# Mixing the values ahead of the gate step in every attention turn

## The chip, the cores and the metric

One core of one Trainium2 chip runs the whole kernel. The metric is the device time of one launch in microseconds, as the median of several runs. Times inside the kernel are read from one profiled execution.

## The reference

Two network blocks stand one behind the other, on 1024 positions of width 1024, in float32. The first block (a convolution mixer and a feed-forward part) and the pooling layer of the second block come before the part that matters here. That part is the attention layer of the second block: 16 query heads of 64 channels, 2 heads of keys and values, a window of 128 positions, a bias by distance and a sink for each head.

```python
q, z = jnp.split(h @ w_in, 2, axis=-1)
q = q * (HEAD_DIM ** -0.5)
...
s = jnp.einsum('bqhgd,bkhd->bhgqk', qn, kn).astype(jnp.float32) + pos_bias
s = jnp.where(mn[None, None, None], s, NEG_INF)
m = jnp.maximum(jnp.max(s, axis=-1, keepdims=True), sink)
p = jnp.exp(s - m)
p = p / (jnp.sum(p, axis=-1, keepdims=True) + jnp.exp(sink - m))
return jnp.einsum('bhgqk,bkhd->bqhgd', p.astype(vn.dtype), vn)
...
return (o * jax.nn.silu(z)) @ w_out
```

So three things come together: the scores and their softmax, the mixing of the values with the probabilities, and the gate z, which is a plain product of the normed stream h with weights.

## The kernel before

The kernel is written with explicit engine programs. Each of TensorE, VectorE, ScalarE, GpSimd and SyncE has its own list of instructions, and they meet only at semaphores (`wait_ge`, `then_inc`). An engine does its list strictly in the written order. A plain product is made of three matmuls for each 128 rows of the contraction (high part by high part, high by low, low by high), 512 columns each.

Attention is cut into 32 windows: for each of the two heads of keys and values, 16 query windows of 64 positions. A loop `for u in range(32 + 4)` on each engine is a pipeline over them. In turn u TensorE does, in this order:

- `scores(u)` (line 1469): 8 matmul instructions, into banks 4 to 7.
- In turns 0 to 2 a tile of queries, `query_pair`.
- `gate_step(n)` for n = u (lines 1453 to 1455): one eighth of a gate tile, three matmuls into bank 3. In turns 4 to 7 there are two such steps, so that from turn 8 on the step number is the turn. A tile is full after eight steps, at the end of the gate steps of turns 7, 15, 23 and 31. The first step of a tile waits until ScalarE has read the tile before (`act_read`).
- `mix_values(u - 4)` (line 1497): four matmuls of 512 columns into bank 2 (two in windows whose first chunk of keys is hidden: windows 0, 1, 16 and 17). The two with the high parts wait for `turned_hi`, the two with the low parts for `turned_split` of their chunk.
- `turn(u - 3)` (line 1481): the transposes of the probabilities, four for each chunk of keys, two chunks (one in windows 0, 1, 16 and 17). Chunk 0 goes to bank 0 and chunk 1 to bank 1, and each chunk increments `turned`.

In turns 32 to 35 there are no scores and no gate steps. Instead `second_gate` makes a whole gate tile of 24 matmuls (lines 1098 to 1100) in each.

ScalarE in turn u: in turns 7, 15, 23 and 31 first the read of the full gate tile (`read_tile`, line 1667); then two copies of the mixed values of window u - 4 (line 2154); then the casts of the transposed chunks of window u - 3 to their high part (line 2159, `turned_hi`); then four exponentials for window u (line 2165). VectorE in turn u: bias, maximum and negation of the scores of window u (`soften`, line 2909), the reciprocal for window u - 1 (line 2947), the sum of the two mixed parts for window u - 4 (line 2918), and the low parts of the chunks of window u - 3 (line 2956, `turned_split`). GpSimd scales the probabilities (line 1071) and in some turns splits weights.

So the probabilities of one window pass from TensorE (transposes, turn u) to ScalarE (high part) to VectorE (low part) and back to TensorE (mixing, turn u + 1).

Of the kernel before, what the change touches and what calls it, by code (L numbers as in the profile page):

```python
# [222 lines left out]
def build(nc, x_in, vec_in, slab_in, ada_in, c_in, rel_in, sink_in, row_scratch, skew_scratch, out):  # L223
# [3 lines left out]
    with root:  # L227
# [218 lines left out]
        def first_chunk(u):  # L446

            return 1 if (u % 16) // 2 == 0 else 0

        def chunks(u, chunk=0):  # L450

            return sum(2 - first_chunk(w) for w in range(u)) + max(0, chunk - first_chunk(u))
# [641 lines left out]
        def _(pe):  # L1094
# [76 lines left out]
            def pair_job(t, g, place, own_base, before, crossed=True, part=range(4)):  # L1171

                order = [(0, 0), (1, 0), (0, 1), (1, 1)] if crossed else [(0, 0), (0, 1), (1, 0), (1, 1)]
                for j in part:
                    n, half = order[j]
                    if j == 0:
                        pe.wait_ge(slab_ready, g + 1)
                    if n == 1 and order[j - 1][0] == 0 and j < 3:
                        pe.wait_ge(slab_ready, g + 2)
                    freed(j, act_read, own_base, before)  # L1180
                    slab_tile(t + j, place + n, half)
# [237 lines left out]
            def query_pair(n, part=range(4)):  # L1419
                g = ATT_SLAB + 2 + 2 * n  # L1420
                pair_job(Q_TILE + 4 * n, g, SLAB_PLACE[g], ATT_ACTS + 4 * n, [(act_read, ATT_ACTS + 4 * n)],
                         crossed=False, part=part)
# [14 lines left out]
            def second_gate(j):  # L1437

                pe.wait_ge(slab_ready, ATT_SLAB + 12 + j // 2 + 1)
                pe.wait_ge(top_done, 4 * (31 + j // 2))  # L1440
                slab_tile(Z_TILE + 4 + j, SLAB_PLACE[ATT_SLAB + 12] + j // 2, j % 2, at=bank[4 + j])

            def gate_step(n):

                tile, k = divmod(n, KT)
                e, half = divmod(tile, 2)
                if k == 0:
                    pe.wait_ge(slab_ready, ATT_SLAB + 10 + e + 1)
                    pe.wait_ge(act_read, Z_ACTS + tile)
                cols = slice(P * k, P * k + P)  # L1450
                place = SLAB_PLACE[ATT_SLAB + 10] + e
                wh, wl, xh, xl = WH[place][:, cols], WL[place][:, cols], HH[:, k, hs(half)], HL[:, k, hs(half)]
                nc.tensor.matmul(bank[3], wh, xh, start=k == 0, stop=False)
                nc.tensor.matmul(bank[3], wh, xl, start=False, stop=False)
                last = nc.tensor.matmul(bank[3], wl, xh, start=False, stop=k == KT - 1)
                if k == KT - 1:
                    last.then_inc(tiles, 1)


            def scores(u):  # L1460
                group, sub = divmod(u, 16)
                if u >= 2:
                    pe.wait_ge(top_done, 4 * (u - 1))
                lo = hidden(u)
                keys = slice(HD * sub - BLOCK + lo, HD * sub + HD)
                for pos in range(4):
                    rows = slice(HD * (pos // 2), HD * (pos // 2) + HD)
                    dst = bank[4 + 2 * (u % 2) + pos // 2]
                    last = nc.tensor.matmul(dst[:, 256 * (pos % 2) + lo:256 * (pos % 2) + WINDOW],
                                            QP[rows, 2 * group + pos % 2, BLOCK * sub:BLOCK * sub + BLOCK],  # L1470
                                            KD[group][rows, keys], start=True, stop=True)
                last.then_inc(scored, 1)

            def turn(u):
                pe.wait_ge(normed, u + 1)
                at = 1 - u % 2
                for chunk in range(first_chunk(u), 2):
                    if u:
                        pe.wait_ge(turned_split, chunks(u - 1, chunk + 1))
                    for pos in range(4):  # L1480
                        last = nc.tensor.transpose(bank[chunk][:, P * pos:P * pos + P],
                                                   PB[u % 4][:, pos, at + BLOCK * chunk:at + BLOCK * chunk + BLOCK],
                                                   ident[:, :])
                    last.then_inc(turned, 1)

            def mix_values(u):

                group, rest = divmod(u, 16)
                blk = rest // 2
                pe.wait_ge(turned_hi, chunks(u + 1))  # L1490
                if u >= 1:
                    pe.wait_ge(o_read, u)
                for part in range(2):
                    for chunk in range(first_chunk(u), 2):
                        if part:
                            pe.wait_ge(turned_split, chunks(u, chunk + 1))
                        last = nc.tensor.matmul(bank[2], V[group][:, blk - 1 + chunk, :], PT[part][:, chunk, :],  # L1497
                                                start=(part, chunk) == (0, first_chunk(u)), stop=(part, chunk) == (1, 1))
                last.then_inc(mixed, 1)


            for u in range(32 + 4):
                if u < 32:
                    scores(u)
                else:
                    second_gate(u - 32)
                if u < 3:
                    query_pair(3, (u + 1,))
                if 4 <= u < 32:
                    for n in ((2 * u - 8, 2 * u - 7) if u < 8 else (u,)):  # L1510
                        gate_step(n)
                if u >= 4:
                    mix_values(u - 4)
                if 3 <= u < 35:
                    if u == 3:
                        pe.wait_ge(act_read, Z_ACTS)
                    turn(u - 3)
# [1576 lines left out]
```

## Time and profile before

| | us |
|---|---|
| median of 3 runs (1972.07 to 1974.19) | 1972.36 |
| the profiled execution's own time | 1973.21 |
| its span, first to last instruction | 1971.5 |
| TensorE busy (matmuls) | 1949.2 (99%) |
| VectorE busy | 1408.7 (71%) |
| GpSimd busy | 891.2 (45%) |
| ScalarE busy | 759.6 (39%) |
| TensorE's mean granted clock | 0.998 of full |

The attention loop's turns 4 to 31 lie between about 1698 and 1800 us of the span. Busy time of TensorE is not TensorE at its peak, since neighbouring matmuls overlap in the records: the distance between the starts of two matmuls is the better measure.

### The profile page before, as it was taken

To read this page: it belongs to the slowest core of one execution; us is meant where nothing else is said; L and a number is where in the kernel's file an instruction comes from. 1 tells how busy PE (TensorE), PEld (TensorE's weight loads), DVE (VectorE), ACT (ScalarE), POOL (GpSimd) and SP (SyncE) were. 2 spreads that over 40 slices of the span, in tenths; PEclk is the share of its full clock that TensorE was granted. 3 is DMA by queue.
4 is the path that set the end of the run, shared out by engine and by line. 5 is a ranking of instruction groups with operands and counts; after the bars stand their busy time and mean duration, and the time that the engine had idled before them with its cause. 6 is when DMAs were issued, how large, how long until landed. Compare 5 with 4: busy or idle time off the path is not lost.

```text
span 1971.5 us, 23476 instructions
## 1 busy us (share of the span) xinstructions
PE 1949.2 (99%) x8916; PEld 1602.3 (81%) x8916; DVE 1408.7 (71%) x2029; ACT 759.6 (39%) x1211; POOL 891.2 (45%) x596
## 2 busy tenths in 40 slices
PE   9999999999999999999999999999999999999998
PEld 7888887788888888888887788878888888777887
DVE  6999677887777776766578777776565580597566
ACT  6323435533333333121165444342122271698112
POOL 4668835645445443222264454432121472454633
PEclk9999999999999999999999999999999999999999
DMA  4231113244455444432013233263332121000202
GB/s 157 83 118 33 47 61 118 91 155 160 155 184 174 150 171 171 158 142 101 28 44 107 84 109 140 76 242 142 118 107 75 43 59 43 22 23 22 75 11 86
DMA packets 63630, 201.21 MB, mean 102 GB/s; under 512 B 7568, under 2 KB 12832, under 8 KB 63520
## 3 DMA queue, kind: packets, MB, share of 16 engines
q1 hardware_dynamic: 51088, 161.50, 23.6%
q10 hardware_dynamic: 12432, 38.23, 5.7%
q8 instruction: 71, 1.16, 0.2%
q14 instruction: 39, 0.32, 0.0%
HBM read 165.08 MB, written 37.77 MB: 103 GB/s over the span
## 4 chain that ended last, share of the span: by engine, by line
PE 84%; DVE 6%; ACT 4%; POOL 3%; issue 2%; DMA 1%; SPq 0%; DVEq 0%; POOLq 0%; ACTq 0%
PE psum L1098 14%; PE psum L1100 14%; PE psum L1099 14%; PE psum L1275 10%; PE psum L1273 10%; PE psum L1274 10%; POOL temp L905 2%; PE psum L1387 1%; PE psum L1386 1%; PE psum L1385 1%; PE psum L1165 1%; ACT probs L2165 1%; PE psum L1167 1%; PE psum L1166 1%; PE psum L1497 1%
## 5 line engine op out<-in xcount | busy, mean ns | idle before, releaser
L870 POOL TENSOR_TENSOR w_lo<-w_raw,w_hi 128x1024 fp32r<-128x1024 f32 x103 | 253.5, 2473 | 428.0 <-ACT w_hi L1597 426.4
L1098 PE MATMUL psum<-norm_hi,w_hi 128*128 128x512 f32 (+1 forms) x752 | 290.5, 386 | 0.0
L1099 PE MATMUL psum<-norm_lo,w_hi 128*128 128x512 f32 (+1 forms) x752 | 289.2, 385 | 0.0
L1100 PE MATMUL psum<-norm_hi,w_lo 128*128 128x512 f32 (+1 forms) x752 | 289.2, 385 | 0.0
L1273 PE MATMUL psum<-norm_hi,w_hi 128*128 128x512 f32 x464 | 181.4, 391 | 0.6 <-DVE temp L2618 0.6
L1275 PE MATMUL psum<-norm_hi,w_lo 128*128 128x512 f32 x464 | 181.2, 391 | 0.0
L1274 PE MATMUL psum<-norm_lo,w_hi 128*128 128x512 f32 x464 | 181.0, 390 | 0.0
L2650 DVE TENSOR_TENSOR stream<-psum,stream 128x512 f32<-128x512 f32 x176 | 121.2, 690 | 78.7 <-PE psum L1100 78.7
L2301 DVE SCALAR_TENSOR_TENSOR stream<-psum,mods,stream 128x512 f32<-128x512 f32 x160 | 118.7, 749 | 81.3 <-PE psum L1100 81.3
L1098 PEld LDWEIGHTS psum<-norm_hi,w_hi 128*128 128x128 f32 x752 | 141.3, 188 | 28.4 <-issue 0.2
L1100 PEld LDWEIGHTS psum<-norm_hi,w_lo 128*128 128x128 f32 x752 | 141.3, 188 | 28.2
L1099 PEld LDWEIGHTS psum<-norm_lo,w_hi 128*128 128x128 f32 x752 | 141.3, 188 | 28.0 <-issue 0.2
L1273 PE MATMUL psum<-sum_hi,w_hi 128*128 128x512 f32 x408 | 159.0, 390 | 3.1 <-DVE sum_lo L2524 1.7
L1275 PE MATMUL psum<-sum_hi,w_lo 128*128 128x512 f32 x408 | 158.7, 389 | 0.0
L1274 PE MATMUL psum<-sum_lo,w_hi 128*128 128x512 f32 x408 | 158.7, 389 | 0.0
L2388 DVE SCALAR_TENSOR_TENSOR psum<-glu,vec,psum 128x1024 f32<-128x1024 f32 x116 | 149.6, 1290 | 4.1
L1597 ACT CAST w_hi<-w_raw 128x1024 fp32r<-128x1024 f32 x86 | 87.8, 1049 | 146.2 <-PE psum L1100 87.9
L2618 DVE TENSOR_TENSOR temp<-psum,temp 128x512 f32<-128x512 f32 x140 | 94.7, 689 | 56.3 <-PE psum L1275 55.7
L1098 PE MATMUL psum<-sum_hi,w_hi 128*128 128x512 f32 x320 | 124.9, 390 | 1.4 <-issue 1.4
L1100 PE MATMUL psum<-sum_hi,w_lo 128*128 128x512 f32 x320 | 124.5, 389 | 0.0
L1099 PE MATMUL psum<-sum_lo,w_hi 128*128 128x512 f32 x320 | 124.5, 389 | 0.0
L1818 ACT CAST w_hi<-second_sum 128x512 fp32r<-128x512 f32 x34 | 21.2, 623 | 214.7 <-POOL second_sum L1007 214.7
(343 smaller groups left out, 4536.6 us busy)
## 6 DMA issues: line engine op xcount, KB each, us to landing
w_raw<-in_slabs SPq DMA_DIRECT2D x141, 512.0 KB, 3.5
ada_raw<-in_ada ACTq DMA_DIRECT2D x27, 1024.0 KB, 5.0
spare_raw<-in_slabs SPq DMA_DIRECT2D x20, 512.0 KB, 4.4
ffn_y_scratch<-ffn_y SPq DMA_DIRECT2D x18, 512.0 KB, 5.0
late_raw<-in_slabs SPq DMA_DIRECT2D x14, 512.0 KB, 3.5
pair_b<-pooled_scratch SPq DMA_DIRECT2D x7, 1024.0 KB, 4.9
pool_gate_scratch<-pair_c SPq DMA_DIRECT2D x12, 512.0 KB, 4.7
sum_raw<-ffn_y_scratch SPq DMA_DIRECT2D x5, 1024.0 KB, 4.9
```

What stands on the lines that cost most here:

```text
L870: nc.gpsimd.tensor_tensor(WL[place][:, :], RAW[at % 2][:, :], WH[place][:, :].bitcast(f32), ALU.subtract).then_inc(slab_ready, 1)
L1098: nc.tensor.matmul(dst, wh, xh, start=n == 0, stop=False)
L1099: nc.tensor.matmul(dst, wh, xl, start=False, stop=False)
L1100: last = nc.tensor.matmul(dst, wl, xh, start=False, stop=n == len(terms) - 1)
L1273: nc.tensor.matmul(dst, wh[:, cols], xh(k), start=k == 0, stop=False)
L1274: nc.tensor.matmul(dst, wh[:, cols], xl(k), start=False, stop=False)
L1275: last = nc.tensor.matmul(dst, wl[:, cols], xh(k), start=False, stop=k == 3)
L1597: nc.scalar.copy(WH[place][:, :], RAW[at % 2][:, :]).then_inc(w_hi_done, 1)
L2301: ins = nc.vector.scalar_tensor_tensor(part, src, mods[:, gate + e:gate + e + 1], part, ALU.mult, ALU.add)
L2388: step(nc.vector.scalar_tensor_tensor(ACC, window, w, ACC, ALU.mult, ALU.add))
L2618: nc.vector.tensor_tensor(dst, src, other, ALU.add).then_inc(part_added, 1)
L2650: nc.vector.tensor_tensor(part, down_bank(j), part, ALU.add).then_inc(dve_read, 1)
```

## The change

TensorE's two steps in the middle of a turn change places. Nothing is added or taken away, no wait is changed, and the other engines' programs stay as they are. After it, the order within a turn is scores, mixing, gate step or steps, transposes.

```diff
                 if u < 3:
                     query_pair(3, (u + 1,))
+                if u >= 4:
+                    mix_values(u - 4)
                 if 4 <= u < 32:
                     for n in ((2 * u - 8, 2 * u - 7) if u < 8 else (u,)):
                         gate_step(n)
-                if u >= 4:
-                    mix_values(u - 4)
                 if 3 <= u < 35:
                     if u == 3:
                         pe.wait_ge(act_read, Z_ACTS)
                     turn(u - 3)
```

## Rows read from the trace of the kernel before

**Rows 1.** Busy time by stage: window, PE, PEld, DVE, ACT, POOL, clock, DMA.
```profile
1712.60:1742.00 29.40, 29.40 (x190) 22.50 (x189) 27.54 (x103) 28.72 (x98) 20.53 (x19) 1.00 0.05 19
...
1799.80:1828.00 28.20, 28.20 (x141) 23.70 (x140) 13.97 (x26) 15.19 (x32) 7.20 (x4) 1.00 0.06 20
```

**Rows 2.** The chain that ended last, in one turn: start, us, what.
```profile
1735.55 1.08 ACT w_hi L2159 x2
1736.62 1.76 ACT probs L2165 x8
1738.41 0.37 ACT q_then_o L2154
```

**Rows 3.** Timeline, turns 14 and 15: start, duration, engine, instruction.
```profile
1737.85 1.03 PE L1481 MATMUL psum<-ident,probs 128*128 128x128 f32 x8
...
1738.82 0.93 PE L1469 MATMUL psum<-keys,q_then_o 64*128 64x192 f32 x8
...
1739.20 1.08 ACT L2159 CAST w_hi<-psum 128x512 fp32r<-128x512 f32 x2
1739.67 0.19 PEld L1453 LDWEIGHTS psum<-norm_hi,w_hi 128*128 128x128 f32 x1 [0.23 <-issue]
...
1739.82 1.29 DVE L2956 TENSOR_TENSOR w_lo<-psum,w_hi 128x512 fp32r<-128x512 f32 x2 [0.16 <-ACT w_hi L2159]
1740.01 0.39 PE L1454 MATMUL psum<-norm_lo,w_hi 128*128 128x512 f32 x1
...
1740.24 0.40 PE L1455 MATMUL psum<-norm_hi,w_lo 128*128 128x512 f32 x1
...
1741.16 0.19 PEld L1497 LDWEIGHTS psum<-w_lo,w_hi 128*128 128x128 f32 x1 [0.26 <-DVE w_lo L2956]
...
1741.50 1.03 PE L1481 MATMUL psum<-ident,probs 128*128 128x128 f32 x8
...
1741.94 0.59 ACT L1667 ACTIVATE gate_raw<-psum 128x512 f32<-128x512 f32 x1
```

**Rows 4.** Timeline, turn 3.
```profile
1697.41 0.66 PE L1481 MATMUL psum<-ident,probs 128*128 128x128 f32 x4
...
1698.11 0.59 ACT L2159 CAST w_hi<-psum 128x512 fp32r<-128x512 f32 x1 [0.84 <-PE psum L1481]
...
1698.99 0.66 DVE L2956 TENSOR_TENSOR w_lo<-psum,w_hi 128x512 fp32r<-128x512 f32 x1
```

**Rows 5.** Timeline, turns 4 to 7.
```profile
1700.83 0.60 PE L1481 MATMUL psum<-ident,probs 128*128 128x128 f32 x4
...
1701.03 0.76 ACT L2154 COPY q_then_o<-psum 64x256 f32<-64x256 f32 x2 [0.56 <-PE psum L1497]
...
1708.60 0.77 ACT L2154 COPY q_then_o<-psum 64x256 f32<-64x256 f32 x2 [0.60 <-PE psum L1497]
...
1709.38 1.08 ACT L2159 CAST w_hi<-psum 128x512 fp32r<-128x512 f32 x2
...
1712.12 0.59 ACT L1667 ACTIVATE gate_raw<-psum 128x512 f32<-128x512 f32 x1
...
1713.62 1.07 ACT L2159 CAST w_hi<-psum 128x512 fp32r<-128x512 f32 x2
```

**Rows 6.** Who waited for whom, 1680 to 1832: total, times, longest.
```profile
ACT q_then_o L2154 <- PE psum L1497: 14.1, 7, 5.4
```

**Rows 7.** Timeline, turns 17 and 18.
```profile
1748.23 0.68 DVE L2956 TENSOR_TENSOR w_lo<-psum,w_hi 128x512 fp32r<-128x512 f32 x1
...
1750.29 1.08 ACT L2159 CAST w_hi<-psum 128x512 fp32r<-128x512 f32 x2
...
1753.84 1.07 ACT L2159 CAST w_hi<-psum 128x512 fp32r<-128x512 f32 x2
```

**Rows 8.** Timeline, the end of turn 31.
```profile
1799.51 1.03 PE L1481 MATMUL psum<-ident,probs 128*128 128x128 f32 x8
...
1800.30 0.48 PE L1098 MATMUL psum<-norm_hi,w_hi 128*128 128x512 f32 x1
```

## The prediction

> **What bounds the kernel now.** I read the page first: TensorE is busy 99% of the span, so a change of its order looks as if it could cost nothing or everything. The stages tell more [rows 1]. In turns 8 to 15 of the attention loop TensorE, VectorE and ScalarE are all busy over nine tenths, while from turn 32 on (1799.8 us) VectorE and ScalarE are half idle and TensorE alone sets the pace. Then the chain of waits through one turn [rows 2]: it runs through ScalarE without a hole, casts 1.08, exponentials 1.76 and copies about 0.8, a period of 3.65 us. So in the full turns ScalarE is the bound, and what TensorE does late matters only where it reaches ScalarE. The timeline of turns 14 and 15 shows how late that is [rows 3].
>
> **TensorE's own pace** [rows 3]. From the start of the transposes it is 0.97 us to the scores (1737.85 to 1738.82), 0.85 to the next step, 0.34 for the first matmul behind the scores, and 0.23 for each further one (1740.01 to 1740.24). With six of those (two gate matmuls and four of mixing) a turn takes 3.54 us. Before and after the change it is the same work, and below ScalarE's 3.65. TensorE has spare time, and it is seen as the wait of the last mixing matmul for VectorE's low part: that part ends at 1739.82 + 1.29 = 1741.11, the weight load comes at 1741.16, the transposes at 1741.50, 0.39 behind the low part.
>
> **What the change does.** The gate step's three matmuls, 3 x 0.23 = 0.69 us, stand now in front of that wait and fill it. After the change they stand behind it, so the transposes start 0.39 + 0.69 = 1.08 us behind the low part. Mixing comes no earlier at its end, because the low part's time decides it. The gate tile, which ScalarE reads every eighth turn, is full later too.
>
> *One steady turn.* A chunk of transposes is ready for ScalarE 0.60 us after their start plus 0.04: four of them take 0.60 [rows 5], and in turn 3, with a slower first one, the cast came at 1698.11 for transposes of 1697.41 + 0.66 = 1698.07 [rows 4]. Before: 1737.85 + 0.64 = 1738.49, used at 1739.20, a slack of 0.71. After: a slack of 0.02. The second chunk is ready 1.07 behind the start and used 0.54 behind the first cast: slack 0.82 before, 0.13 after. The closed loop, from cast to cast, is 0.62 to the low part's start, 1.29 for it, 1.08 to the transposes, 0.64 to the next cast: 3.63 us against ScalarE's 3.65. So the steady turns cost nothing, but only just. The other consumer is VectorE, which wants the next scores: they move from 1738.82 + 0.93 = 1739.75 to 1740.44, and it is busy with low parts until 1741.11, so 0.6 us are left there. Queued behind the mixing on TensorE are only the gate step, the transposes and the next scores. No DMA and no SyncE or GpSimd instruction is moved, and GpSimd's scaled probabilities lie a turn ahead.
>
> *Turns 4 to 7, two gate steps each.* Here 1.39 us stand behind the wait, and the loop is 0.62 + 1.29 + 0.39 + 1.39 + 0.64 = 4.33 us, over TensorE's present 3.54 + 0.69 = 4.23 in these turns. I follow it. The low part of window 0 ends at 1698.99 + 0.66 = 1699.65 [rows 4]; transposes of window 1 at +0.39 + 1.39 = 1701.43 (before 1700.83 [rows 5]). Window 1 has one chunk: cast 1702.07, low part 1702.69 to 1703.38, transposes of window 2 at 1705.16. Cast 1705.80, low part to 1707.71, transposes of window 3 at 1709.49. Cast 1710.13, against 1709.38 before [rows 5]: 0.75 late. Low part to 1712.04, gate steps 6 and 7 until the last one starts at 1713.59 and ends, at 0.40, at 1713.99. Now ScalarE must read that tile before its copies and casts: at 1714.03, against 1712.12 [rows 5]. The read (0.59) takes 0.62 to the copies and these (0.76) take 0.78 to the cast, with 0.01 of rounding: 1715.44, against 1713.62. **Term 1: +1.82 us**, which ScalarE, without slack from here on, carries along.
>
> *Turns 15 and 23, the next full tiles.* The gate step now ends at the low part's end + 0.39 + 0.69 + 0.17, and ScalarE can read 0.04 later: 1741.11 + 1.29 = 1742.40 against 1741.94 [rows 3], 0.46 late, and with 0.02 lost at the casts behind it 0.48. **Term 2: 2 x 0.48 = +0.96.** The read in turn 31 delays only ScalarE, which is no longer the bound.
>
> *Turns 17 and 18.* The exponentials of window 16 are short (64 columns), so ScalarE comes early and TensorE is the bound now. With 0.48 from turn 15, window 13's low part ends at 1748.91 + 0.48 = 1749.39 [rows 7], the transposes of window 14 start 0.40 + 0.69 later, at 1750.48, and the cast comes at 1751.12, not 1750.29 [rows 7]: 0.83, so 0.35 more. The next one by the same loop: 1751.12 + 3.63 = 1754.75 against 1753.84, 0.91. **Term 3: 0.35 + 0.08 = +0.43.** From window 16 on ScalarE keeps that distance.
>
> *The end.* After turn 31 TensorE alone is the bound. It enters turn 32 at 1800.30, 0.79 behind the transposes' start at 1799.51 [rows 8]. These now start one gate step later. **Term 4: +0.69.** From there nothing gives anything back, since mixing and transposes in turns 32 to 35 lie between whole gate tiles, and both other engines wait for TensorE.
>
> Sum: 1.82 + 0.96 + 0.43 + 0.69 = +3.90 us. The profiled execution took 1973.21, its span of 1971.5 and 1.71 around it, and would take 1977.1. The median of the three runs lies 0.85 below it, and 1972.36 + 3.90 = **1976.3 us**, +0.20%.
>
> The price of a gate matmul decides this sum: the rows say 0.23 us from start to start [rows 3]. The Trainium skill, page "TensorE: Matmul & The Clock Gate", section "Back-to-back issue gap", gives a sustained 131 ns for 512 columns, and N / 2.4 + 2.5 ns, so 216 ns, for an isolated one. By the first, a gate step would be 0.39 us, and the sum, as an estimate, would shrink to about 0.8 us, for turns 4 to 7 would keep their pace. The trace agrees with the second and I take its 0.23.
>
> **The rivals.**
> *Hidden after all (not slower).* ScalarE idles before its copies in turns 4 to 6, 0.56 us in the first and 0.60 in the last [rows 5]. If the earlier start of mixing gives it that time back, and it reaches the tile read of turn 7 no later than before, term 1 goes and with it most of term 3. Then 0.96 + 0.69 = 1.65 us stay, 1974.0, or term 4 alone, 1973.1. It decides where the read of turn 7 comes before about 1712.8. Against it: in these turns the transposes wait for low part and gate steps, whatever ScalarE does.
> *A cheaper gate step.* If the gate matmuls, all queued behind one wait, followed one another as closely as the transposes do (1.03 / 8 = 0.13 us [rows 3]), terms 1 and 3 would vanish, term 2 be 2 x 0.18 and term 4 be 0.39: +0.8, 1973.1. The 0.23 between gate matmuls speaks against it. The section "Back-to-back issue gap" of the Trainium skill's page on TensorE would have it so by its first figure.
> *The loop becomes the bound.* The slack of 0.02 is smaller than what I know of the 0.64. If the first chunk is released later, each 0.1 us costs 0.1 - 0.02 in some 22 full turns, 1.8 us. At the far end, were it as late as the second chunk (1.07, not 0.64), the loop would be 4.06 and cost 0.41 x 22 = 9 us: 1985. A moderate case is 1978 to 1979. For it: the margin. Against it: the same 0.04 stands behind every other group of matmuls.
> *Faster.* Mixing starts earlier where the low part was long done, so ScalarE's copies come earlier. It waited seven times for mixing, 14.1 us in all and up to 5.4 at once [rows 6], but the long ones lie in turns 32 to 35, between whole gate tiles that stay in place. In turns 4 to 6 there are three of at most 0.60 [rows 5]: 1.8 us can be won, 1970.6, and only if the later transposes cost nothing.
> Lower than nothing is excluded for the steady turns by ScalarE's full program; the clock granted is 1.00 in all these stretches, and TensorE does the same work per turn.
>
> **How the numbers follow.** My forecast, with +3.2 to +4.7 us, gets 0.68; hidden 0.13; cheaper gate step 0.02; loop bound 0.13; faster 0.04. About 0.2%, 3.9 us, is what a measurement of this kernel tells from no change, and my sum lies on that line, so its 0.68 is split: 0.31 below and 0.37 above, since the unknown of the steady turns can only add. With hidden, cheaper and most of faster, "same" gets 0.49 and "slower" 0.37 + 0.13 = 0.50; faster by over 0.2% has 0.01, for no row offers 3.9 us. The range leaves out the lowest part of hidden and faster and the far end of the loop: 1973.4 to 1979.0. The forecast's own range is 1975.5 to 1977.1.
>
> **What would show it.** In the changed kernel's timeline: transposes 1.08 us behind the low part in full turns and casts still every 3.65 us (3.7 or more: the loop's rival); the tile read of turn 7 some 1.9 us later than before, with ScalarE idle in front of it; short idle times of ScalarE before the reads of turns 15 and 23 and before the casts of windows 14 and 15; turn 32 entered 3.9 us later; and no difference from there to the end but that shift. The prediction is wrong if TensorE's records show another order of waits, if a chunk is released later than 0.64 behind its start, or if a later stage gives the delay back.

## The result: 0.21% slower, and where the profile after shows it

The changed kernel took 1977.04 us (median of 11 runs, 1976.25 to 1980.07) against 1972.84 for the kernel before on the same chip (11 runs). The ratio is 1.0021, with a 95% interval of 1.0013 to 1.0029. That is +4.1 us, between +2.6 and +5.7; forecast were +3.9. The profiled span went from 1971.5 to 1975.6 us, and the mean granted clock is 0.997, against 0.998 before.

Single executions also differ ahead of the loop: window 0's cast comes at 1695.16 us in one profile of this case (e2, below) and at 1699.00 in another (e10). So the loop is measured by itself in every profile: **loop time** is from the start of window 0's cast on ScalarE (turn 3) to the first matmul of turn 32. In the profile of before it is 1698.11 [rows 4] to 1800.30 [rows 8], 102.19 us. After the change it is 1698.64 to 1804.43, 105.79 us. From there to the last instruction it is 171.12 us, against 171.19 before, so nothing behind the loop gives the delay back.

The first lines are the timeline of the changed kernel in one of its full turns (turn 10), where before had the gate step ahead of the wait [rows 3].

```profile
1723.86 1.29 DVE L2956 TENSOR_TENSOR w_lo<-psum,w_hi 128x512 fp32r<-128x512 f32 x2 [0.15 <-ACT w_hi L2159]
...
1725.54 0.40 PE L1453 MATMUL psum<-norm_hi,w_hi 128*128 128x512 f32 x1
...
1726.23 1.03 PE L1481 MATMUL psum<-ident,probs 128*128 128x128 f32 x8
...
1726.88 1.07 ACT L2159 CAST w_hi<-psum 128x512 fp32r<-128x512 f32 x2
```

The low part ends at 1725.15, the gate step follows 0.39 us later, and the transposes stand 1.08 behind the low part, as forecast. The cast starts 0.65 us behind the transposes, and 0.64 of that is the forecast's time to the end of the first four. So 0.01 us is left of the slack of 0.71: ScalarE and TensorE arrive together. The chain of waits says it in another way. Here are four entries of it in the changed kernel; the chain does not leave TensorE in these turns, where it ran through ScalarE before [rows 2].

```profile
1726.39 0.87 PE psum L1481 x8
1727.27 0.86 PE psum L1469 x8
1728.12 1.22 PE psum L1497 x4
...
1729.81 0.23 PE psum L1455
```

The period is 3.64 us all the same. A reader of the chain alone would say that TensorE is now the bound and costs something in each of these turns, and that is not so: two loops of nearly equal length run side by side, and the chain names one of them. (Where ScalarE's own turn is shorter, at windows 14 and 15, the casts of the changed kernel come every 3.63 us; that is the other loop's own pace.)

Turn 7 of the changed kernel is the dearest place. These lines of its timeline answer to [rows 5].

```profile
1711.29 1.29 DVE L2956 TENSOR_TENSOR w_lo<-psum,w_hi 128x512 fp32r<-128x512 f32 x2 [0.85 <-ACT w_hi L2159]
...
1712.97 0.40 PE L1453 MATMUL psum<-norm_hi,w_hi 128*128 128x512 f32 x1
1713.20 0.39 PE L1454 MATMUL psum<-norm_lo,w_hi 128*128 128x512 f32 x1
...
1713.44 0.39 PE L1455 MATMUL psum<-norm_hi,w_lo 128*128 128x512 f32 x1
...
1714.12 0.39 PE L1455 MATMUL psum<-norm_hi,w_lo 128*128 128x512 f32 x1
...
1714.35 1.03 PE L1481 MATMUL psum<-ident,probs 128*128 128x128 f32 x8
1714.54 0.60 ACT L1667 ACTIVATE gate_raw<-psum 128x512 f32<-128x512 f32 x1 [1.04 <-PE psum L1455]
1715.17 0.76 ACT L2154 COPY q_then_o<-psum 64x256 f32<-64x256 f32 x2
...
1715.95 1.07 ACT L2159 CAST w_hi<-psum 128x512 fp32r<-128x512 f32 x2
```

The low part ends at 1712.58, six gate matmuls follow 0.39 us later, and ScalarE idles 1.04 us for a full tile. It reads the tile 15.90 us behind the cast of window 0, where before it was 14.01 (1712.12 [rows 5]), so 1.89 later. Its cast starts at 1715.95, or 17.31 behind the cast of window 0. Before it was 15.51 (1698.11 [rows 4] to 1713.62 [rows 5]). The other places are seen in its table of waits, from 1690 to 1804 us:

```profile
ACT w_hi L2159 <- PE psum L1481: 3.6, 6, 0.8
...
ACT gate_raw L1667 <- PE psum L1455: 1.4, 2, 1.0
...
ACT keys L1667 <- PE psum L1455: 0.7, 2, 0.4
```

ScalarE waits six times for transposes, where before it waited once (for 0.8 us, in turn 3), and four times for a full gate tile (the third and fourth are written to a tile named keys); of the second kind there was none before.

### The profile page after: what moved, and what is told of

Read it like the earlier page. It is cut to its first block, busy times and chain, and to the rows that moved or that the text cites. A ratio compares the mean times of both kernels' runs of the same rounds, so it can differ in the third digit from the quotient of the medians.

```text
span 1975.6 us, 23476 instructions
## 1 busy us (share of the span) xinstructions
PE 1951.1 (99%) x8916; PEld 1603.1 (81%) x8916; DVE 1408.4 (71%) x2029; ACT 758.4 (38%) x1211; POOL 891.8 (45%) x596
## 4 chain that ended last, share of the span: by engine, by line
PE 87%; DVE 5%; POOL 3%; ACT 2%; issue 2%; DMA 0%; SPq 0%; DVEq 0%; POOLq 0%; ACTq 0%
PE psum L1098 14%; PE psum L1100 14%; PE psum L1099 14%; PE psum L1273 10%; PE psum L1274 10%; PE psum L1275 10%; POOL temp L905 2%; PE psum L1497 2%; PE psum L1385 1%; PE psum L1387 1%; PE psum L1386 1%; PE psum L1165 1%; PE psum L1167 1%; PE psum L1166 1%; PE psum L1481 1%
```

## The experiments

All loop times below are of one profile each. The kernel before was profiled again (label e10_before_again) and showed 101.86 us, 0.33 less than its first profile: its full turns took 3.64 us, not 3.655. All other profiles show 3.64 where ScalarE sets the pace. So all differences are taken from 101.86, which makes the changed kernel +3.93. Against the first profile, from which the forecast was made, it is +3.60, and every other difference is 0.33 smaller too. Ratios are to the kernel before in the same series of runs. The texts written ahead of e1 to e8 count loop time from the first scores of turn 4, by which it is 102.30 in the first profile of before, so their differences are what to compare with the table, not their absolute figures.

| kernel | loop time | over 101.86 | ratio of times (95%) |
|---|---|---|---|
| e10, before again | 101.86 | 0 | 1.0000 (0.9991 to 1.0009) |
| the change | 105.79 | +3.93 | 1.0021 (1.0013 to 1.0029) |
| e1, turns 4 to 7 alone | 103.69 | +1.83 | 1.0011 (1.0002 to 1.0020) |
| e2, turns 8 to 31 alone | 104.00 | +2.14 | 1.0013 (1.0004 to 1.0022) |
| e3, all but the tile-filling turns | 104.00 | +2.14 | 1.0014 (1.0005 to 1.0023) |
| e4, change, tile read behind casts | 104.27 | +2.41 | 1.0013 (1.0004 to 1.0022) |
| e9, turn 31 alone | 102.63 | +0.77 | 1.0001 (0.9992 to 1.0010) |
| e5, gate step inside mixing | 107.71 | +5.85 | 1.0030 (1.0018 to 1.0041) |
| e11, one gate matmul inside mixing | 102.23 | +0.37 | 1.0001 (0.9992 to 1.0010) |
| e6, change, a fourth matmul | 110.85 | +8.99 | 1.0052 (1.0037 to 1.0068) |
| e7, before, a fourth matmul | 104.29 | +2.43 | 1.0011 (1.0002 to 1.0021) |
| e8, even deal of the gate matmuls | 100.67 | -1.19 | 0.9991 (0.9982 to 1.0000) |
| e12, even deal and the change | 105.64 | +3.78 | 1.0016 (1.0007 to 1.0025) |

**Which turns: e1, e2.** The new order under a condition:

```diff
-                if u >= 4:
+                if u >= 4 and u < 8:          # e2: u >= 8
                     mix_values(u - 4)
...
                         gate_step(n)
+                if u >= 4 and not (u < 8):    # e2: not (u >= 8)
+                    mix_values(u - 4)
```

> Loop time here means the time from the first scores matmul of turn 4 to the first matmul of turn 32: 102.30 us before (1698.00 to 1800.30), 105.89 us after the whole change (1698.54 to 1804.43). Only turns 4 to 7, those with two gate steps, have the new order. My theory: two steps behind the low part stretch these turns to 4.33 us, and the gate tile's read in turn 7 comes late, so ScalarE loses some 1.8 us there and keeps the loss: loop time 104.1, time +1.8 us over before. Rival (hidden at the entry, the whole loss is one of the later turns): loop time 102.3 to 102.6, time as before.

> Only turns 8 to 31, with one gate step each, have the new order. My theory: nothing in the steady turns, but 0.48 at each of the two reads of a full tile (turns 15 and 23), 0.43 behind the short exponentials (windows 14 and 15) and 0.69 at the end: loop time 104.1 to 104.4, time +1.8 to +2.1 us over before, and the sum of this and of the run with turns 4 to 7 alone is the whole change. Rival (hidden at the entry): loop time 105.6 or more, time +3.3 or more.

Measured: +1.83 and +2.14, together 3.97 for the whole change's 3.93. In e1 window 4's cast comes 17.28 us behind window 0's, as in the changed kernel; in e2 it comes at 15.50, as before. The loss at the entry is real and half of the whole, and the rival that hides it is refuted.

**The tile-filling turns: e3, and the end: e9.**

```diff
-                if u >= 4:
+                if u >= 4 and u not in (7, 15, 23, 31):           # e9: u == 31
                     mix_values(u - 4)
...
                         gate_step(n)
+                if u >= 4 and not (u not in (7, 15, 23, 31)):     # e9: not (u == 31)
+                    mix_values(u - 4)
```

> The new order in all turns but 7, 15, 23 and 31, those that fill a gate tile. My theory: the reads of turns 15 and 23 cost nothing, the end costs nothing, and in turn 7 ScalarE loses 1.07 instead of 1.82 (the read at about 1713.0 and the copies at 1713.9 of the unshifted trace). With 0.43 for windows 14 and 15 the loop time is 103.6 to 103.8, time +1.3 to +1.5 us over before. Rival (the loss comes from the steady turns and not from the tile's reads and the end): loop time 105 or more, for 24 of 28 turns are as in the changed kernel.

> The new order in turn 31 alone, the last with a gate step. Loop time is taken from the cast of window 0 to the first matmul of turn 32: 102.19 us in the profile before. My theory (term 4): the transposes of turn 31 start 1.08 us behind the low part, not 0.39, and turn 32 is entered 0.69 later than in a profile of the kernel before whose steady period is the same: loop time 102.5 to 102.9. Rival (TensorE catches up inside the turn): 101.9 to 102.2.

Measured: e9 cost +0.77 in the loop, 0.71 of it from window 27's cast on, near the 0.69; its ratio of times alone would not tell it from nothing. e3 cost +2.14, against 1.3 to 1.5 expected. Its parts: window 4's cast 1.04 late (1.07 expected), the windows 14 and 15 0.44, the two tile reads nothing, as expected; but 0.60 at the end, where I had nothing. The timeline of e3 in turns 30 and 31 shows why:

```profile
1798.59 1.04 PE L1481 MATMUL psum<-ident,probs 128*128 128x128 f32 x8
1799.55 0.93 PE L1469 MATMUL psum<-keys,q_then_o 64*128 64x192 f32 x8
1800.41 0.50 PE L1453 MATMUL psum<-norm_hi,w_hi 128*128 128x512 f32 x1
...
1802.14 1.04 PE L1481 MATMUL psum<-ident,probs 128*128 128x128 f32 x8
1802.93 0.48 PE L1098 MATMUL psum<-norm_hi,w_hi 128*128 128x512 f32 x1
```

From transposes to transposes it is 3.55 us, the forecast's pace of TensorE without any wait (3.54). TensorE came out of turn 30 late by a gate step, and one turn of old order gives back only what its pace is shorter than ScalarE's, 0.1 us. Term 4 is a lag of TensorE that the changed turns keep up, and not a matter of the last turn.

**The late tile read: e4.**

```diff
-                if u in (7, 15, 23, 31):
-                    n = (7, 15, 23, 31).index(u)
-                    read_tile((Z_TILE + n, 3), ZR[n // 2][:, hs(n % 2)])
...
                         nc.scalar.copy(PT[0][:, chunk, :], bank[chunk]).then_inc(turned_hi, 1)
+                if u in (7, 15, 23, 31):
+                    n = (7, 15, 23, 31).index(u)
+                    read_tile((Z_TILE + n, 3), ZR[n // 2][:, hs(n % 2)])
```

> The whole change, and on ScalarE the read of a full gate tile moved behind the casts of its turn, so that a late tile stops nothing in front of them. My theory: the casts of turn 7 wait for their transposes only (ready at 1714.46 in the unshifted trace) and the reads of turns 15 and 23 cost about 0.1 each: 1.5 + 0.2 + 0.43 + 0.69 = 2.8, less what the steady turns won (0.2): loop time 104.9, 1.0 us shorter than the change alone. Rival (the late tile read costs nothing by itself, only the late transposes do): loop time 105.9 as with the change alone.

Measured: 104.27, 1.5 us shorter than the change. Window 4's cast is 16.29 behind window 0's: 0.78 more than before, late for its transposes; 0.84 was expected. The next one is 4.12 later, 0.48 more than in a full turn, because the read stands there now: 1.26 in all for the entry, against 1.80. At the other two reads the loss is gone altogether (0.1 each expected). So 0.54 + 2 x 0.48 = 1.5 us of the change is the late tile in front of ScalarE's other work. The rival is refuted.

**The closed loop's margin: e6, e7.** The second product of each gate step from step 8 on is done twice, so that product stands twice in the sums of these gate tiles.

```diff
                 nc.tensor.matmul(bank[3], wh, xl, start=False, stop=False)
+                if n >= 8:
+                    nc.tensor.matmul(bank[3], wh, xl, start=False, stop=False)
                 last = nc.tensor.matmul(bank[3], wl, xh, start=False, stop=k == KT - 1)
```

> The whole change, and each gate step of turns 8 to 31 has a fourth matmul (its second one twice), so the gate tiles of the reads in turns 15, 23 and 31 have wrong sums: 24 more matmuls of 0.23 us, 5.5 us of TensorE. My theory: the closed loop of low part, gate step, transposes and cast is at its limit (3.64 us), so each turn pays nearly all of a matmul: 4.6 to 5.5 us over the changed kernel, casts every 3.85 to 3.87 us. Rival (TensorE's own program with its 0.11 us of slack per turn is what sets the pace): 0.12 per turn, 2.8 us over the changed kernel.

> The kernel before with the same fourth matmul in each gate step of turns 8 to 31 (same wrong sums). My theory: there the extra matmul first fills TensorE's wait of about 0.11 us per turn, and the rest lengthens the turn to TensorE's own pace, 3.54 + 0.23 = 3.77 us: 0.12 in some 21 turns and all 0.23 in turns 16 to 18 where TensorE is the bound: 2.9 to 3.4 us over before, against 4.6 to 5.5 for the same work in the changed order. Rival (an extra matmul costs the same in both orders, for TensorE is 99% busy): 5.5 us in both.

Measured: in the changed order +5.06 us (110.85 to 105.79), casts every 3.86 us, both as expected; TensorE's 0.11 us of slack does not help there. In the old order the same 24 matmuls cost 2.43, less than the 2.9 to 3.4 of my theory. ScalarE's timeline in e7 shows what I left out:

```profile
1715.39 0.76 ACT L2156 COPY q_then_o<-psum 64x256 f32<-64x256 f32 x2 [0.17 <-PE psum L1499]
...
1774.85 0.37 ACT L2156 COPY q_then_o<-psum 64x256 f32<-64x256 f32 x1
1775.24 1.07 ACT L2161 CAST w_hi<-psum 128x512 fp32r<-128x512 f32 x2
1778.10 0.76 ACT L2156 COPY q_then_o<-psum 64x256 f32<-64x256 f32 x2
...
1782.52 1.08 ACT L2161 CAST w_hi<-psum 128x512 fp32r<-128x512 f32 x2
1785.43 0.76 ACT L2156 COPY q_then_o<-psum 64x256 f32<-64x256 f32 x2
1786.21 1.07 ACT L2161 CAST w_hi<-psum 128x512 fp32r<-128x512 f32 x2
1789.22 0.76 ACT L2156 COPY q_then_o<-psum 64x256 f32<-64x256 f32 x2 [0.17 <-PE psum L1499]
1790.01 1.07 ACT L2161 CAST w_hi<-psum 128x512 fp32r<-128x512 f32 x2
```

1775.24 to 1782.52 is two turns of 3.64, at ScalarE's pace, though a turn that TensorE bounds is 3.79 in e7 (turns 8 to 14). Only then do the turns grow (3.69, 3.80), with ScalarE waiting. So there is a stock of lead, and TensorE spends it at 0.13 a turn. But ScalarE does not wait for the transposes: it waits for the end of mixing, in front of its copies. From the transposes' start to their cast it is 1.34 us in turn 24 and 0.98 from turn 27 on, so only 0.36 of the 0.71 us [rows 3] can be spent in this way. The change could spend all 0.71, because it makes the transposes later and leaves the end of mixing where it was. These are two paths with a stock of their own, and my theory had neither.

The stock is filled where something else holds ScalarE up, as the tile reads of turns 15 and 23 do. Turns 15, 16 and 20 to 26 of e7 cost next to nothing. Where there is none the price is paid at once: 1.03 us in turns 8 to 14, which follow the double steps, 0.36 in turns 18 and 19, 0.51 in turns 27 to 30, and 0.49 from window 27's cast to turn 32.

**The gate step inside mixing: e5, e11.**

```diff
                 if u >= 4:
-                    mix_values(u - 4)
+                    mix_values(u - 4, 0)          # the matmuls with the high parts
...
                         gate_step(n)
+                if u >= 4:
+                    mix_values(u - 4, 1)          # those with the low parts
```

In e11 two of each gate step's matmuls stand ahead of the first half, and one between the halves.

> The gate steps stand in the middle of mixing: behind the two matmuls with the high parts, ahead of the two with the low parts. Loop time is 102.30 us before and 105.89 after the change, from the first scores of turn 4 to the first matmul of turn 32. My theory: only what stands behind the wait for the low part costs. Here the gate step fills that wait again, TensorE only idles until the high parts are there, and the transposes start some 0.4 us later than before and 0.25 earlier than in the changed kernel: loop time 102.4 to 103.1, time +0.1 to +0.8 us over before. Rival (starting to mix ahead of the gate step is what costs, wherever the gate step stands): loop time 105 or more.

> Of each gate step two matmuls stand ahead of mixing and only the third between its high and its low parts. With all three there, ScalarE's copies of the mixed values became the bound: 1.13 us from cast to first mixing matmul, 1.72 to the transposes, 0.20 to the copies and 0.79 to the next cast, a loop of 3.84 us. Theory (that loop): without two of the matmuls it is 3.38 us, under ScalarE's 3.64, so the cost is gone: loop time 101.8 to 102.6, time as before. Rival (that mixing is cut in two is what costs, whatever stands between): casts still every 3.7 us or more and loop time over 104.

Measured in e5: +5.85, the worst order of all, where +0.1 to +0.8 was expected. My theory, as it stood there, is refuted: it counted only what stands behind the wait for the low part. The time fits the rival. What makes it so, the chain of waits of e5 shows; it is a loop of its own:

```profile
1730.06 0.11 ACT w_hi L2162
1730.17 0.37 issue
1730.54 0.60 ACT w_hi L2162
1731.14 0.04 issue
1731.19 0.73 PE psum L1497 x2
1731.91 0.23 PE psum L1453
1732.15 0.23 PE psum L1454
1732.38 0.23 PE psum L1455
1732.61 0.48 PE psum L1497 x2
1733.11 0.37 ACT q_then_o L2157
...
1733.90 0.11 ACT w_hi L2162
```

From cast to cast it is 3.84 us: both casts, mixing's first half, the gate step, the second half, ScalarE's copies of the mixed values, and the next cast. The copies stand in front of the casts on ScalarE, so the end of mixing counts as much as the transposes do. In the changed order mixing ends when it did before; in e5 the gate step also delays that. With two matmuls taken out of the gap (e11), the loop of 3.38 us no longer binds and casts come every 3.64 again: +0.37, time as before. So the cut of mixing costs next to nothing by itself, and the loop of e5 was the cause.

**Even deal: e8, e12.** Where the change cost most, two whole gate steps stood in one turn. e8 keeps the order of before and deals the 96 matmuls out singly; ScalarE's tile reads move to turns 10, 17, 24 and 31:

```diff
-                if 4 <= u < 32:
-                    for n in ((2 * u - 8, 2 * u - 7) if u < 8 else (u,)):
-                        gate_step(n)
+                for m in range(GATE_ENDS[u - 4], GATE_ENDS[u - 3]) if 4 <= u < 32 else ():
+                    gate_product(m)
...
+GATE_EXTRA = {4: 2, 5: 1, 11: 1, 13: 1, 15: 1, 20: 1, 21: 1, 23: 1, 25: 1, 27: 1, 29: 1}
+GATE_ENDS = [sum(3 + GATE_EXTRA.get(w, 0) for w in range(4, u)) for u in range(4, 33)]
```

> The order of before, but the 96 gate matmuls are dealt out evenly: three a turn and one more in eleven places (two more in turn 4), so that tiles are full in turns 10, 17, 24 and 31, and no turn has two whole steps; ScalarE's reads move with them. My theory: turns 4 to 7 are bound by TensorE (4.23 us) only because of the double steps, and now go at ScalarE's 3.65; the single extra matmuls elsewhere hide in the 0.11 us of slack of their and the next turn. Loop time 101.0 to 101.4 (102.30 before), time 0.9 to 1.3 us under before. Rival (no slack in the later turns): loop time 102.3 or more.

> The even deal of the gate matmuls (tiles full in turns 10, 17, 24 and 31) together with the changed order. From the cast of window 0 to that of window 4 it is 17.31 us in the changed kernel, with one read of a tile (0.62) in it, 15.51 before, also with the read, and 13.93 in the even deal with the order of before, without it. Theory (term 1 came from the double steps behind the low part): with five and four matmuls in turns 4 and 5 and three in 6 and 7 the order costs 0.3 there, 14.2 to 14.3 us. The rest of the loop pays 0.2 for each turn with a fourth matmul, 0.48 for each tile read, 0.43 and 0.69 as before: loop time about 105.1, 4.5 over the even deal in the order of before. Rival (term 1 came from the late read in turn 7 alone, so it is gone here altogether, and the fourth matmuls hide): 13.9 for the first part, loop time 102.8 or less.

Measured: e8 has a loop of 100.67 us, 1.19 under that of before, from which it was expected 0.9 to 1.3 shorter, and a ratio of 0.9991 (0.9982 to 1.0000): in the loop the gain is plain (it is more than three times what the two profiles of before differ by), while in the whole time the interval reaches 1.0000. It is the one version here with a shorter loop than before. Most of the gain is in turns 4 to 7: 13.93 us from window 0's cast to window 4's, against 15.50. e12, the same deal in the changed order: 14.29 us from window 0's cast to window 4's, as expected (14.2 to 14.3), against 13.93 in e8. Term 1 has shrunk to 0.36 us, all of it in turns 4 and 5, which have five and four matmuls; turns 6 and 7, with three, take 3.64 each in both. Without double steps the late transposes cost little. The read of the tile has left these turns too, so e12 alone does not divide term 1 between them; e4 does. But the loop is 105.64, 4.97 over e8 (4.5 expected), since the order without slack pays for the single extra matmuls that e8 hides. The rival (102.8 or less) is refuted.

**The kernel before again: e10.**

> The kernel before, unchanged, to see what a profile and a comparison give where nothing differs. The full turns' casts came every 3.655 us in the profile before and every 3.64 in those of all changed kernels, in turns of old order too. Theory 1: that is a difference from one execution to the next, and this profile may show 3.64 and a loop time near 101.9. Theory 2: it belongs to the order of before: 3.655 and 102.2 again. The ratio of times is 1.000 within its interval in both.

Measured: casts every 3.64 us, loop time 101.86, ratio 1.0000 (0.9991 to 1.0009). The first theory holds.

## Why the prediction was right, by its own steps

It put the time at 1976.3 by +3.90 over the kernel before, and the measured ratio gives +4.1 (2.6 to 5.7). The median of 1977.04 is 0.7 above the forecast, and 0.5 of that is the kernel before, which had 1972.84 over eleven runs and not 1972.36. The loop grew by 3.93. That the sum fits to 0.03 us is in part luck: against the first profile it grew by 3.60, since that one's full turns were slower. The terms fit one by one, and they carry the argument. By its terms, changed kernel against the second profile of before, each as a stretch between two casts:

| term | forecast | measured |
|---|---|---|
| 1, entry, window 0's cast to window 4's | 1.82 | 17.31 - 15.51 = 1.80 |
| 2, tile reads of turns 15 and 23 | 0.96 | 0.48 + 0.47 = 0.95 |
| 3, windows 14 and 15 | 0.43 | 0.35 + 0.07 = 0.42 |
| 4, window 27's cast to turn 32 | 0.69 | 3.78 - 3.09 = 0.69 |
| steady turns | 0 | the rest, 0.07 |

*The bound and the slack.* ScalarE's program is the bound in full turns and the transposes had 0.71 us of slack, which the change used up without paying. The table shows it, and e6 against e7 bears it out: the same extra matmuls cost 5.06 us where the slack is used up and 2.43 where it is not. That the old order had 0.71 us to spare holds only for what delays the transposes alone; for work that delays mixing too it was 0.36 (e7).

*Term 1.* The price and the mechanism hold (e1, e12). The hand-made timetable put the casts of windows 1, 2, 3 and 4 at 3.96, 7.69, 12.02 and 17.33 us behind window 0's; they came at 3.96, 7.70, 12.03 and 17.31. It has two parts, the late transposes and the late tile read in front of the copies; e4 took 0.54 of its 1.80 away by moving the read.

*Term 2* is shown by e3 and e4: without the late tile, or with its read moved, nothing is left of it.

*Term 3* came in size and place. e1, with the old order there, has none of it; e2 and e3, with the new order there, have 0.44, e3 without a loss at the tile reads.

*Term 4.* The size is right, shown by e9. The reason given, that the last transposes start a gate step later, is too narrow: e3, whose last turn has the old order, pays 0.60 as well, for the lag of the turns ahead.

*The price of a gate matmul.* It is 0.23 us in the changed order too (1712.97, 1713.20, 1713.44 in the timeline of turn 7). The sustained 131 ns of the Trainium skill ("TensorE: Matmul & The Clock Gate", section "Back-to-back issue gap") would have given +0.8 us in all, as an estimate; the measurement decides against it here, and its 216 ns for an isolated matmul is the nearer figure.

*The rivals.* Hidden after all: refuted by e1. Cheaper gate step: refuted by the rows of turn 7. The loop as the bound: its margin was as small as feared, 3.63 us in windows 14 and 15 against ScalarE's 3.64, but it held; the steady turns cost 0.07 us together. Faster: the copies in turns 4 to 6 did come without their waits, and the casts behind them then waited for the transposes instead.

What the argument lacked showed only in the experiments: it had one loop through the transposes and none through ScalarE's copies, which this change did not touch and e5 and e7 did.

## What to carry to other kernels

In a pipeline over several engines, ask of each consumer of TensorE's results, and for each result by itself, how long it lies ready before it is used: a step may be moved ahead of it at no cost until that stock is gone, and from then on it costs in full, also where the consumer meets the late result ahead of its other work. A stock may be smaller by another path, and empty just behind a stretch in which TensorE was the bound. Fill a wait with work that nobody needs soon, and keep that work ahead of the wait; here it cost 3.9 us behind it and 5.9 between the parts of mixing. Where there is a slack, work that must be dealt out over turns is best dealt out in small pieces, since a double portion in one turn exceeds a slack that single ones fit (e8); where there is none, the single pieces are paid for too (e12).

## What the runs showed of the hardware

The same kernel ran its full turns at 3.655 us in one profiled execution and at 3.640 in another, 102.19 and 101.86 us for the loop. The difference is in the turns that ScalarE bounds: the stretch from window 0's cast to window 4's, which TensorE bounds, is 15.51 and 15.50, and the 171.19 us behind the loop are the same, while ScalarE's exponentials over 193 columns took 458 ns in the one and 455 in the other (mean, 1716 to 1745 us). Why ScalarE differed is not known. It is as large as the smallest effect here (e11, 0.37), so such stretches should be compared with a second profile of the same kernel.
